# Setup that only turns x, a first norm as a stage of its own, and conditioning gathered in one PSUM bank

## What is computed

```python
for l in range(DEPTH):                     # DEPTH = 2
    sh_m, sc_m, gt_m, sh_f, sc_f, gt_f = split(silu(c) @ w_ada[l] + b_ada[l], 6)         # conditioning
    csh_m, csc_m, cgt_m, csh_f, csc_f, cgt_f = split(silu(c_ctx) @ w_ada[l] + b_ada[l], 6)
    f_lat = mixer_features(modulate(rms_norm(x, g_pre_mix[l]), sh_m, sc_m), ...)
    f_ctx = mixer_features(modulate(rms_norm(xc, g_pre_mix[l]), csh_m, csc_m), ...)
    ...                                    # attention, linear recurrence, output projection, MLP

rms_norm(x, g) = x * rsqrt(mean(x * x) + EPS) * g
modulate(h, shift, scale) = h * (1 + scale) + shift
mixer_features: h @ w_in, then rms_norm of the parts, rotary embedding (tables cos, sin), w_q_up, w_kv_up
```

## Time and profile before

| | us |
|---|---|
| median of 3 runs (lowest, highest) | 4018.92 (4018.32, 4020.68) |
| the profiled execution's own time | 4019.63 |
| its span in the profile | 4017.8 |
| PE, DVE, ACT, POOL busy in the span | 3478.3, 2081.4, 1188.7, 770.7 |
| DMA of `set_wada`, 4 x 2048 KB on ACT's queue, from issue to landing (median) | 21.6 |
| DMA of `pre_wada`, 20 x 2048 KB on SP's queue, from issue to landing (median) | 8.2 |
| DMA of `xin`, 8 x 512 KB on SP's queue, from issue to landing (median) | 6.7 |
| mean granted clock of PE (1.0 is 2.4 GHz, 0.5 is 1.2 GHz) | 0.918 |

### The profile page before, as it was taken

How to read it: one execution, slowest core, us unless ns; L and a number is a source line. 1 busy time by engine, 2 the same in 40 slices (tenths; PEclk the granted TensorE clock), 3 DMA queues, 4 the chain that set the end, 5 groups by cost and what they waited for, 6 DMA issues and landing times. The chain is left out here.

```text
span 4017.8 us, 45956 instructions
## 1 busy us (share of the span) xinstructions
PE 3478.3 (87%) x18921; PEld 1737.7 (43%) x18921; DVE 2081.4 (52%) x3439; ACT 1188.7 (30%) x1629; POOL 770.7 (19%) x386
## 2 busy tenths in 40 slices
PE   5798456789989999999998798449799899999997
PEld 2555342322335555555554545333223365444444
DVE  4681786656634533333335782877666354333334
ACT  2221234334344311111113332334244443122212
POOL 0000560068750000000000000630488500000000
PEclk8898677789999999999999898668799999999998
DMA  5210004400012011111110210023100221111111
GB/s 198 64 32 4 1 1 160 153 11 11 1 55 77 22 43 39 41 43 42 43 32 28 78 43 4 1 76 126 42 1 1 58 63 48 53 48 53 53 48 42
DMA packets 216306, 194.48 MB, mean 48 GB/s; under 512 B 10343, under 2 KB 180386, under 8 KB 216098
## 3 DMA queue, kind: packets, MB, share of 16 engines
q1 hardware_dynamic: 211938, 183.16, 14.9%
q10 hardware_dynamic: 4160, 8.39, 0.6%
HBM read 167.74 MB, written 14.68 MB: 45 GB/s over the span
## 5 line engine op out<-in xcount | busy, mean ns | idle before, releaser
L719 PE MATMUL feed_acc<-feed_aa,feed_w 128*128 128x512 f16 (+1 forms) x3936 | 763.0, 355 | 0.0
L719 PE MATMUL feed_acc<-hh,feed_w 128*128 128x512 f16 (+1 forms) x3936 | 753.6, 354 | 5.2 <-DVE feed_w L1001 5.2
L719 PEld LDWEIGHTS feed_acc<-feed_aa,feed_w 128*128 128x128 f16 x3936 | 388.6, 99 | 377.2 <-issue 15.3
L719 PEld LDWEIGHTS feed_acc<-hh,feed_w 128*128 128x128 f16 x3936 | 385.8, 98 | 370.0 <-DVE feed_w L1001 5.8
L1997 POOL TENSOR_TENSOR at_accp<-at_accp,at_p 128x1024 f32<-128x1024 f32 x192 | 451.3, 2350 | 82.8 <-ACT at_p L2030 74.1
L355 PE MATMUL in_acc<-hh,in_w 128*128 128x512 f16 (+1 forms) x2088 | 399.8, 354 | 64.9 <-DVE in_w L345 52.4
L2051 DVE TENSOR_REDUCE at_mx<-at_small 128x1 f32<-128x512 f32 (+1 forms) x492 | 317.1, 686 | 256.1 <-PE at_small L2107 253.5
L2030 ACT ACTIVATE at_p<-at_sT 128x1024 f32<-128x1024 f32 x246 | 251.9, 1024 | 366.8 <-PE at_sT L2136 366.8
L355 PEld LDWEIGHTS in_acc<-hh,in_w 128*128 128x128 f16 (+1 forms) x2088 | 208.0, 100 | 254.9 <-DVE in_w L345 53.2
L1060 DVE SCALAR_TENSOR_TENSOR y<-feed_acc,y 128x1280 f32<-128x1280 f32 (+1 forms) x96 | 130.3, 1358 | 331.5 <-PE feed_acc L719 331.5
L1047 DVE TENSOR_TENSOR feed_r<-feed_r 128x1280 f32<-128x1280 f32 (+1 forms) x56 | 76.1, 1359 | 418.7 <-ACT feed_r L854 418.7
(11 more groups left out here) (283 smaller groups left out, 4250.2 us busy)
## 6 DMA issues: line engine op xcount, KB each, us to landing
pre<-in_w_ff SPq DMA_DIRECT2D x84, 512.0 KB, 4.0
pre_wada<-in_w_ada SPq DMA_DIRECT2D x20, 2048.0 KB, 8.2
feed_stage<-in_w_ff SPq DMA_DIRECT2D x44, 512.0 KB, 3.9
in_stage<-in_w_in SPq DMA_DIRECT2D x36, 512.0 KB, 4.2
set_wada<-in_w_ada ACTq DMA_DIRECT2D x4, 2048.0 KB, 21.6
pre<-in_w_out SPq DMA_DIRECT2D x12, 512.0 KB, 4.8
x<-x_scratch SPq DMA_DIRECT2D x3, 2048.0 KB, 10.7
xin<-in_x SPq DMA_DIRECT2D x8, 512.0 KB, 6.7
```

The costliest lines, as they stand in the source:

```text
L719: last = nc.tensor.matmul(out[:, b:b + cn], w[:, wh, k, m0:m0 + P], src[:, sh, k, a + b:a + b + cn], start=(k == 0 and wh == 0 and sh == 0 ...
```

## The change

The change has four parts.

**Setup.** All ten tiles of x have a buffer of their own, so SP issues them without waiting. The four groups of conditioning leave the block; the object `A` is handed to both blocks.

**First norm.** `first_norm` takes the place of `between`. SP issues the four conditioning loads at the start of this block, and the three stores of x when the third load has landed. The norm goes by the class `Norms`: two DVE operations per row. PE does all sums, then `rows` four times and `cols` once; ACT copies once; DVE finishes the conditioning after the roots of chunks 0 and 1, and then goes through the rows of chunks 0, 1 and 2.

**Conditioning in one bank** (all users of `Ada`). The padded vectors have 62 columns, with the two values at 30 and 31. `rows` of group j reads columns 30-2j to 62-2j, so that its two results come out at partitions 2j and 2j+1 of each group of 32, and zeros are added to all others. All groups add up in one bank, so there is one `copy` and one `cols` (4 matmuls of 32 columns) in place of one per group, and `rows` waits for no copy.

**`prepare`.** The tables come in the order `sums`, `cast`, cos, sin_b, cos_b, sin, up weights; PE's first matmul waits for `sums` alone. ACT does the second four squares before it waits for cos, and the root before cos of aq, `spin` and the up weights' high parts. DVE's low parts of the up weights move from before the mean to behind item 3. A group of conditioning comes at every fourth item; `copy` follows at item 4n, `cols` at item 4n+2.

```diff
@@ class Ada @@
-        self.c = st.enter_context(nc.sbuf_tensor(nm + "cpad", [P, KT, 32], F32))
+        self.c = st.enter_context(nc.sbuf_tensor(nm + "cpad", [P, KT, 62], F32))
-        self.acc = st.enter_context(nc.psum_tensor(nm + "ada", [P, 48, 2], F32))
+        self.acc = st.enter_context(nc.psum_tensor(nm + "ada", [P, 4, 32], F32))
-        self.nc.vector.tensor_copy(self.c[:, :, 0:2], self.e.cact[:, :, :]).then_inc(self.s_pad, 1)
+        self.nc.vector.tensor_copy(self.c[:, :, 30:32], self.e.cact[:, :, :]).then_inc(self.s_pad, 1)
     def rows(self, pe, j):
         pe.wait_ge(self.s_load[j % self.ring], 16 * (j // self.ring + 1))
-        if j:
-            pe.wait_ge(self.s_copied, j)
-        else:
+        if j == 0:
             pe.wait_ge(self.s_pad, 2)
         for k in range(KT):
             g = 32 * (k % 4)
-            last = self.nc.tensor.matmul(self.row[g:g + 32, :], self.c[:, k, :], self.w[:, j % self.ring, k, :],
-                                         start=(k < 4), stop=(k >= 4), tile_position=(0, g))
+            last = self.nc.tensor.matmul(self.row[g:g + 32, :], self.c[:, k, 30 - 2 * j:62 - 2 * j],
+                                         self.w[:, j % self.ring, k, :], start=(j == 0 and k < 4),
+                                         stop=(j == self.n - 1 and k >= 4), tile_position=(0, g))
         last.then_inc(self.s_used, 1)
-    def copy(self, act, j):
-        act.wait_ge(self.s_used, j + 1)
-        if j:
-            act.wait_ge(self.s_cols, j)
+    def copy(self, act):
+        act.wait_ge(self.s_used, self.n)
-    def cols(self, pe, j):
-        pe.wait_ge(self.s_copied, j + 1)
+    def cols(self, pe):
+        pe.wait_ge(self.s_copied, 1)
         for m in range(4):
-            last = self.nc.tensor.matmul(self.acc[:, 4 * self.groups[j][1] + m, :], self.part[:, m * P:(m + 1) * P],
-                                         self.e.sel[:, :], start=True, stop=True)
+            last = self.nc.tensor.matmul(self.acc[:, m, :], self.part[:, m * P:(m + 1) * P], self.e.sel[:, :],
+                                         start=True, stop=True)
@@ setup_phase @@
-        xin = sb("xin", [P, 4, D])
+        xin = sb("xin", [P, TT, D])
                 for t in range(TT):
-                    if t >= 4:
-                        sp.wait_ge(s_tp, 2 * (t - 3))
-                    sp.dma_start(xin[:, t % 4, :], src).then_inc(s_xin[t % 4], 16)
+                    sp.dma_start(xin[:, t, :], src).then_inc(s_xin[t], 16)
-                for j in range(A.n):
-                    A.load(act, j)
-                for j in range(A.n):
-                    A.copy(act, j)
-                A.finish(dve, ch, 0, 0, 4)
-                    if i >= 8 and i % 3 == 2 and i // 3 - 2 < A.n:
-                        A.rows(pe, i // 3 - 2)
-                    if i >= 10 and i % 3 == 1 and i // 3 - 3 < A.n:
-                        A.cols(pe, i // 3 - 3)
@@ between goes, first_norm comes (its engines whole) @@
+            def _(sp):
+                for j in range(A.n):
+                    A.load(sp, j)
+                sp.wait_ge(A.s_load[A.n - 2], 16)
+                for a, n in cks:
+                    sp.dma_start(e.x_dram[:, :, a:a + n], x[:, :, a:a + n]).then_inc(s_st, 16)
+                sp.wait_ge(s_st, 16 * NC)
+            def _(act):
+                for k in range(KT):
+                    N.square(act, "x", 0, k)
+                for c in range(NC):
+                    if c + 1 < NC:
+                        for k in range(4):
+                            N.square(act, "x", c + 1, k)
+                    if c < 2:
+                        N.root(act, "x", c)
+                    if c + 1 < NC:
+                        for k in range(4, KT):
+                            N.square(act, "x", c + 1, k)
+                A.copy(act)
+                N.high(act, mod, 0, 0, KT)
+                N.root(act, "x", 2)
+                N.high(act, mod, 1, 0, KT)
+                N.high(act, mod, 2, 0, KT)
+            def _(pe):
+                for c in range(NC):
+                    for k in range(KT):
+                        N.add(pe, "x", c, k)
+                for j in range(A.n):
+                    A.rows(pe, j)
+                A.cols(pe)
+            def _(dve):
+                N.average(dve, "x", 0)
+                N.newton(dve, "x", 0)
+                N.average(dve, "x", 1)
+                N.newton(dve, "x", 1)
+                A.finish(dve, ch, 0, 0, 4)
+                ch.wait(dve)
+                N.scale(dve, mod, 0, 0, KT)
+                N.average(dve, "x", 2)
+                N.newton(dve, "x", 2)
+                N.scale(dve, mod, 1, 0, KT)
+                N.scale(dve, mod, 2, 0, KT)
@@ prepare @@
-        turn_at = {2 + 5 * j: j for j in range(ada.n)}
+        turn_at = {2 + 4 * j: j for j in range(ada.n)}
+        turned = 4 * ada.n
@@ prepare, ACT @@
                 evacuate(0)
-                act.wait_ge(s_ca, 32)
+                for q in range(4, 8):
+                    square(0, q)
+                act.wait_ge(s_ca, 16)
                 nc.scalar.activation(cos["ak"], cos["aq"], ACT.Copy, scale=...).then_inc(s_cos, 1)
+                root(0)
...
-                for q in range(4, 8):
-                    square(0, q)
...
-                root(0)
...
-                    if i in turn_at:
-                        ada.copy(act, turn_at[i])
+                    if i == turned:
+                        ada.copy(act)
@@ prepare, PE @@
-                pe.wait_ge(s_sel, 32)
+                pe.wait_ge(s_sel, 16)
...
                     if i in turn_at:
-                        if turn_at[i]:
-                            ada.cols(pe, turn_at[i] - 1)
                         ada.rows(pe, turn_at[i])
-                ada.cols(pe, ada.n - 1)
+                    if i == turned + 2:
+                        ada.cols(pe)
@@ prepare, DVE: from before mean(0) to behind item 3 @@
+                    if i == 3:
+                        for q, (R, j, n) in enumerate(parts):
+                            dve.wait_ge(s_uh, q + 1)
+                            nc.vector.scalar_tensor_tensor(uw[0:R, 1, j, 0:n], up[0:R, j, 0:n], WSCALE,
+                                                           uw[0:R, 0, j, 0:n], ALU.mult, ALU.subtract).then_inc(s_ul, 1)
```

196 lines of the change are left out of this document (40 added, 156 removed).

## The result

| | before | changed |
|---|---|---|
| median of the runs, us | 4018.91 (4018.32 to 4020.68) | 3974.48 (3970.47 to 3977.94) |
| ratio, 95% interval | | 0.9888 (0.9871 to 0.9906) |
| span of the profiled execution | 4017.8 | 3968.7 |
| PE, DVE, ACT busy | 3478.3, 2081.4, 1188.7 | 3439.3, 2073.5, 1180.3 |

The changed kernel's runs spread over 7.5 us, and its profiled execution is the shortest of them. So I profiled it a second time (run changed_again, span 3976.4), and the stages stand here from both. A stage goes from the first DMA or first operation of one block to that of the next.

The account below looks back on a forecast made before the run. PE bounds most of the program, but the touched stretches are held by whichever engine is full, DVE or PE. Front 16.8 + 2 x 2.5 + 6.7 + 3.5 = 32.0 off 4019.63 gives 3987.6, median 3987; range 3977 to 3998.

Parts of the forecast that it names:

- Setup: Setup: all 20 copies of x go 0.95 us apart, so it takes 36.9 us in place of 56.7, 19.8 earlier.
- First norm: First norm, now with the conditioning in it: DVE idle 56.2 to 67.8, then two-operation rows; 61.6 us long, ending at 98.5.
- Rival 1: First norm: conditioning is late, by `rows` at half clock (+5.6) or a late fourth load; front -11, 3993 us; chance 0.17.
- Start of `prepare`: Start of `prepare`, both layers: `sums` issued first lets PE start sooner, 4.1 us earlier; net -2.5 per layer after +1.6.
- The lows: `prepare`, behind item 3: the up weights' low parts, formerly in a wait, now cost DVE 1.6 us per layer.
- Groups, layer 0: `prepare` of layer 0: less PE conditioning work saves 6 us in the third chunk and 0.7 in the first two, -6.7.
- rival 2: `prepare`: PE does not hold the third chunk, only early tables gain, 5 + 3 in place of 15; 3995 us; chance 0.12.
- Groups, layer 1: `prepare` of layer 1: fewer `cols` in the second chunk (6.8 us for 11.9) and none at the end, -3.5.
- Rival 4: `prepare`: with fewer groups PE idles more and falls to the low clock, up to 49 us more, 4036; chance 0.03.
- Rival 3: `prepare`: all PE time of the groups is on the path and the low parts are free, 42 off, 3978; chance 0.12.

Follow-up runs that it names:

- tables_only: Kernel before with only the start of `prepare` changed (table load order, squares and root ahead, lows later), conditioning as before: 4008.86 us, ratio 0.9976.
- lows_twice: Changed kernel with the up weights' three low parts computed a second time into a spare buffer, right behind the first: 3973.04 us, ratio 0.9886.
- bank_only: Kernel before with only `prepare`'s conditioning changed: one bank, one copy and turn near the end, a group every 4th item: 4001.85 us, ratio 0.9958.
- bank_every5: Kernel before with one-bank conditioning in `prepare`, one turn at the end, but groups still after every 5th item: ratio 0.9984.
- idle_work_before: Kernel before with three unused 128x384 matmuls after items 5, 9, 10 and 18 of the second chunk of `prepare`: ratio 0.9990.
- prepare_only: Kernel before with the change's whole `prepare`, but the old setup and first norm: 3994.15 us, ratio 0.9940.

## Why the prediction was wrong

- **Setup** (-19.8 predicted, -22.5 and -23.1 found). The step that failed is the pace: "that is how all 20 go now". The 0.95 us were PE at its lower level, although the clock column said 1.00. PE worked without a break from 18.32 to 25.62 us and its loads got fast at 24.2, and from there DVE's 0.71 to 0.75 holds. The last copy ended at 33.7 and not 36.1.
- **First norm** (+3.0 predicted, +3.6 and +3.7 found). The total was near partly by luck, since two errors cancel. The second mean came 17.4 us after the block's start and not 15.1: PE's eight sums of chunk 1 took 7.13 us at the full clock, where 4.8 were left for them. The four `rows` took 7.07 and not 9. Scaling thus began 31.6 us after the start for a forecast 30.9, and the rest took 30.6 for 30.7. Rival 1 fell: DVE was released by PE, `rows` were warm, no DMA. The two-operation rows took 0.66 from start to start.
- **Start of `prepare`** (-4.1 predicted; found, from the first issue to DVE's `bkv`, -5.05 and -4.66 in the two layers). Up to the spread by `cast`, 5.0 us were gained in layer 0 for the 4.1 counted: the landing took 2.4 us and not 3, and the second four sums 4.24 and not 4.8. The step from there to `bkv` is as long as before (6.0).
- **The lows** (+1.6 predicted). They do stand in full in DVE's busy time (41.18 against 39.63), but the chunk they stand in does not show them clearly in tables_only: 1.1 us longer in layer 0, 0.8 shorter in layer 1. Over both layers no cost is seen, where 3.2 us were counted; with chunks that vary by 1.5 us, and lows_twice undecided, their price stays open.
- **Groups, layer 0** (-6.7 predicted, -14.6 found in bank_only). This is the step that was wrong in substance. The third chunk was close: 6 counted, 4.7 found, so rival 2 fell. For the first two chunks the prediction says "I count 0.7"; found 9.9, of which 7.3 in the second, where the full-clock work of the groups did not shrink (11.7 and 11.5). I summed PE's instructions at the full clock in a stretch whose own row said 0.71. (Eight `rows` and seven `cols` are also 22.7 by the prices given, not 22.4, which changes nothing.) Two things were missed in the second chunk: taking the turns away is worth 4.4 us there at the low clock (bank_every5), and keeping the clock up 3.0 more. Taken alone in the kernel before, the clock is worth 5.6, with nothing removed and 8.6 us of work added (idle_work_before). The 2.6 us of the first chunk (clock 0.99 for 0.94) were not taken apart.
- **Groups, layer 1** (-3.5 predicted, -3.8 found in bank_only). With the tables in too, 7.3 and 10.4 us were found for 6.0; in six profiles of kernels with this `prepare` the stage took 125.8 to 128.9 us, longer where the clock of its second chunk was lower (0.84 to 0.98). That part is spread, and why one execution has it and another not stays open.
- **Rival 4** had the right mechanism and the wrong sign: I asked whether fewer fillers lower the clock, and not whether ones spaced more closely raise it. **Rival 3** had nearly the right time (3978) for half the right reason: the turns' PE time is on the path in part, and the low parts show no clear cost.
- The unchanged in-projection and recurrence of layer 0 were 2.1 us shorter in the first profile and 0.1 in the second: spread, not an effect.

Of the 12 us, 3 are the setup's pace, of which the first norm takes back 0.6, and 8 are `prepare` (prepare_only: 23.5 for 15.2), most of it in the second chunk of layer 0, by the clock and the turns; the spread of the runs covers the rest.

## What to carry to other kernels

Where a stretch of the kernel before shows a lower clock, its instructions must not be summed at the full one: look what PE did ahead of it, and price the change as if the clock could come back. Small PE work that is due at no fixed time belongs into the gaps of a stretch that another engine fills, evenly; where it is not to be had, idle work can be cheaper than the gap (layer 0), but it costs time where the clock was high already (layer 1). And a DMA that is issued early, while others are under way, can hold the engine that issues it, and with it the end of the stage.
